# Modulation weights of a two-block network: from running weighted sums over input rows to dot products along the rows of outputs

## The chip, the cores and the metric

The kernel runs on one core of one Trainium2 chip, in float32 throughout. The metric is device time in microseconds (us) of one execution. Large products are made on TensorE with each weight split into a high part (`whi`, fp32r) and a low part (`wlo`); VectorE and ScalarE make the splits.

## The reference, cut to what matters

Two blocks follow each other. Each turns a condition vector into six vectors of 2048 numbers ("modulation": shifts, scales and gates), and uses them around its products. In the second block (the first is alike, with `w_ada`, `b_ada`):

```
sh_m, sc_m, gt_m, sh_f, sc_f, gt_f = split(silu(c) @ w_mod + b_mod, 6)
csh_m, csc_m, ...                  = split(silu(c_ctx) @ w_mod + b_mod, 6)
h_lat = rms_norm(x, norm_mix_g) * (1 + sc_m) + sh_m      # 256 latent tokens
h_ctx = rms_norm(ctx, norm_mix_g) * (1 + csc_m) + csh_m  # 256 context tokens
... mixer of h_lat and h_ctx ...
x = x + gt_m * (mixed @ w_out)
x = x + gt_f * swiglu(rms_norm(x, norm_ffn_g) * (1 + sc_f) + sh_f)
```

`w_ada` and `w_mod` are 2048 x 12288. Each is read once and multiplied with one or two vectors; from the context's condition only the first two of the six vectors are used. The mixer of block one is a state-space scan with pooling and Fourier branches, that of block two a gated linear scan (8 heads) and windowed attention (8 heads).

## The kernel before, in words

A planner (`schedule`) writes one list of "beats" for the whole program, and each engine runs the beats that name it, in that order. The main stream is the weights of the large products: SyncE loads pieces of 128x1024 (`raw`), ScalarE rounds each to `whi` (L1373), VectorE subtracts for `wlo` (L1800), and TensorE makes three matmuls per 128x128 block: `wlo`, `whi`, `whi` (L883). There are four `raw` buffers and three split buffers; a piece's split starts when the piece three before it has been used up. With a moving side of 256 columns a piece is 8 blocks.

Beside it runs a background stream, `mods`. `Plan.flowed` counts the columns that TensorE has been given and, whenever the background's pace is reached (4.7, 5.7, 4.2 and 6.0 in the four stages, in units close to a microsecond of TensorE), puts one step of `mods` into the list. What is said here holds for the 20 halves that it makes: in block one the vectors j = 2, 3, 4 (stage (0, 2), during the gates), then j = 5 (stage (0, 5), during the first feed-forward's gate and up products), in block two j = 0, 1 (stage (1, 0), until well into that feed-forward), j = 2, 3, 4 (stage (1, 2), during the scan and the attention) and j = 5 (stage (1, 5)). j = 0, 1 of block one are made at the start by other code, which the change leaves alone.

For each vector j and each half of its 2048 outputs, `mods` takes 16 pieces of 128 inputs x 1024 outputs. GpSimd loads each through its own queue (L847, a ring of two buffers). VectorE multiplies the piece by the 128 condition values that stand one per partition (`csil`, in `misc`), and adds it to an accumulator of 128x1024: `TENSOR_SCALAR` for the first (L1812), `SCALAR_TENSOR_TENSOR` for the other 15 (L1731, a helper's line). For j = 0, 1 of block two there are two conditions and so two accumulators: two instructions a piece. After the 16 pieces `modsum` sums over the partitions on TensorE: 8 products of a 128x128 block of the accumulator with one column of ones, into a PSUM tile of 128x8 ("ps<-cst,t ... 128x1"; the profile names its constant operand first, and shows two matmul records for each). VectorE adds the bias and writes `mv` (L1822, `modv<-ps,small`). `modsum` stands in TensorE's order like any other work, and what follows it there waits. Its PSUM tile comes from the ring `s.aux`, which has one bank in stages (0, 5) and (1, 0), two or four elsewhere.

ScalarE's part ahead of the change is only the `Silu` of the four condition vectors at the very start, on 128x16 each.

Of the kernel before, what the change touches and what calls it, by code (L numbers as in the profile page):

```python
# [11 lines left out]
P = 128  # L12
# [20 lines left out]
for _n, _w in [("b_ada", 96), ("norm_mix_w", 16), ("norm_ffn_w", 16), ("conv_w", 120), ("conv_b", 24),  # L33
               ("d_skip", 32), ("ssd_norm_w", 16), ("pool_scale", 16), ("final_norm_w", 16), ("c", 16),
# [3 lines left out]
    _small(_n, _w)  # L38
# [18 lines left out]

class Plan:


    def __init__(self):
# [3 lines left out]
        self.back, self.modded = iter(()), set()  # L65
# [81 lines left out]
def mods(s, layer, js):  # L147
    for j in js:
        for half in range(2):
            for k in range(KT):  # L150
                s.add("mod", layer, j, half, k)
                yield
            yield
            s.add("modsum", layer, j, half, s.aux)
        s.modded.add((layer, j))
        if j < 2:
            s.modded.add((layer, j + 6))
# [67 lines left out]
def schedule():  # L225
# [119 lines left out]
    def ctx2():  # L345
        s.need(1, 1)
# [216 lines left out]
class Dry:  # L563
# [6 lines left out]
    scalar_tensor_tensor = tensor_copy = reciprocal = memset = tensor_reduce = tensor_tensor_scan = dma_start = _none  # L570
# [16 lines left out]
def build(nc, A, out):  # L587
    ctx = ExitStack()
    with ctx:
# [4 lines left out]
        "rc_in rs_in am_in stored zero hi lo used pool_mm ada_pe ada_sum rms_pe mods_pe tr_pe dt_pe ssd_pe pf_pe hg_pe at_pe "  # L594
        "init_v ada_v mod_v start_v conv_v dt_v ssd_v pf_v merge_v res_v norm_v ffn_v hg_v at_v mat_v "
        "silu_a start_a sq_a conv_a tok_a dt_a ssd_a z_a pf_a gate_a norm_a ffn_a val_a hg_a at_a").split()


def program(nc, A, out, ctx):
# [23 lines left out]
    csil = misc[:, 16:80].rearrange("p (v k) -> p v k", v=4)  # L623
# [73 lines left out]
    mod_rings, accs = {}, {}  # L697

    def mod_memory(stage, after, n, n_acc):
        mod_rings[stage] = [Buf(carve(PIECE), f"w{i}", after) for i in range(n)]  # L700
        accs[stage] = [carve(PIECE) for _ in range(n_acc)]

    mod_memory((0, 2), f2, 2, 1)
# [13 lines left out]
    mod_memory((0, 5), f3, 2, 2)  # L717
    mod_rings[1, 0], accs[1, 0] = mod_rings[0, 5], accs[0, 5]
    c2sq = ring(1, lambda: carve(PIECE), f3)
# [6 lines left out]
    mod_memory((1, 2), f5, 2, 1)  # L726
# [36 lines left out]
    mod_memory((1, 5), f7, 2, 1)  # L763
# [9 lines left out]
    acc_bufs = {st: [Buf(a, None, f) for a in accs[st]] for st, f in (((0, 2), f2), ((0, 5), f3), ((1, 2), f5), ((1, 5), f7))}  # L773
    acc_bufs[1, 0] = acc_bufs[0, 5]
# [12 lines left out]

    def mod_stage(layer, j):
        return (layer, j) if (layer, j) in mod_rings else (layer, 2 if j > 1 else 0)
# [47 lines left out]
    def pool(e):  # L837
# [3 lines left out]
        def mod(layer, j, half, k):  # L841
            w = A["w_ada"] if layer == 0 else A["w_mod_2"]
            b = S.take(mod_rings[mod_stage(layer, j)], "mod", layer, j, half, k)
            S.free("mod", layer, j, half, k, by=("mod_v", "acc2" if j < 2 else "acc", layer, j, half, k))
            a = j * D + half * PIECE
            g.wait_ge(*S.freed("mod", layer, j, half, k))
            e.dma_start(b, w[k * P:(k + 1) * P, a:a + PIECE]).then_inc(*up(S.sem("mod", layer, j, half, k), layer, j, half, k, n=16))  # L847
# [28 lines left out]
        run(beats, {"mod": mod, "pf_load": pf_load, "ctx2": ctx2, "hg_in": hg_in})  # L876

    def pe(e):
# [156 lines left out]

        def modsum(layer, j, half, ring):
            for i in range(2 if j < 2 else 1):
                S.take(rings[ring], "mods", layer, j, half, i)
                acc = accs[mod_stage(layer, j)][i]
                g.wait_ge(*S.freed("mods", layer, j, half, i), *at("mod_v", "acc2" if i else "acc", layer, j, half, KT - 1))  # L1040
                ps = S.buf("mods", layer, j, half, i)
                for m in range(8):
                    ins = mm(ps[:, m:m + 1], acc[:, m * P:(m + 1) * P], ones[:, 0:1])
                ins.then_inc(*up("mods_pe", layer, j, half, i))
# [273 lines left out]
        run(beats, {"ada": ada, "ada_sum": ada_sum, "ada_tr": ada_tr, "rms_in": rms_in, "mm": product, "pool": pooled, "modsum": modsum, "btok": btok, "xtok": xtok, "dt": dt, "ssd": ssd,  # L1318
# [3 lines left out]
    def act(e):  # L1322
# [14 lines left out]
        for v, name in enumerate(("c", "c_ctx", "c_2", "c_ctx_2")):  # L1337
# [381 lines left out]
        run(beats, {"rms_in": rms_in, "ada_sum": ada_sum, "ada_h": ada_h, "stage": stage, "silu": silu, "btok": btok, "xtok": xtok, "ev_dt": ev_dt, "dt": dt, "ssd": ssd, "ev_z": ev_z,  # L1719
# [5 lines left out]
    def dve(e):  # L1725
# [76 lines left out]
        def mod(layer, j, half, k):  # L1802
            b, st = S.buf("mod", layer, j, half, k), mod_stage(layer, j)
            g.wait_ge(*at(S.sem("mod", layer, j, half, k), layer, j, half, k))
            for i in range(2 if j < 2 else 1):
                acc, cv, key = accs[st][i], csil[:, 2 * layer + i, k:k + 1], ("acc", "acc2")[i]
                if k == 0:
# [683 lines left out]
```

## Time and profile before

| | |
|---|---|
| median of 3 runs | 3573.88 us (3573.77 to 3575.22) |
| the profiled execution | 3571.92 us, span 3570.1 us |
| busy: TensorE | 3438.3 us, 96% of the span |
| busy: VectorE | 2375.5 us, 67% |
| busy: ScalarE | 1540.5 us, 43% |
| busy: GpSimd | 180.1 us, 5% |
| granted TensorE clock, mean | 0.984 of full speed |

PE is TensorE's matmuls, PEld its weight loads, DVE is VectorE, ACT ScalarE, POOL GpSimd, SP SyncE. The span starts with the first instruction and ends with the last; 1.8 us of the execution lie outside it.

### The profile page before, as it was taken

How to read it: one execution, taken by the hardware profiler on the slowest of the kernel's cores; microseconds unless marked ns; L12 is line 12 of the kernel's file. 1: busy time of each engine (PE TensorE's matmuls, PEld its weight loads, DVE VectorE, ACT ScalarE, POOL GpSimd, SP SyncE). 2: the span in 40 equal slices, each digit the busy share in tenths (PEclk: the TensorE clock that was granted, in tenths of full speed). 3: DMA queues.
4: the chain of work that ended last, by engine and by line, in shares of the span. 5: the costliest groups of instructions: out<-in, count | busy, mean ns of one | idle time of the engine just before them, and what ended most of it. 6: DMA issues, size and time to landing. Idle time of an engine off the chain costs nothing. (4 is left out here: it accounts for less than half of the span.)

```text
span 3570.1 us, 59053 instructions
## 1 busy us (share of the span) xinstructions
PE 3438.3 (96%) x25176; PEld 3196.5 (90%) x25176; DVE 2375.5 (67%) x3028; ACT 1540.5 (43%) x2174; POOL 180.1 (5%) x342
## 2 busy tenths in 40 slices
PE   7889999899999999999999999999988999999999
PEld 3477788699999989999999989999887899999999
DVE  6876666456777776688776566766696666445544
ACT  2244545434333344433433444555454444334443
POOL 0000000000001000000000001001000000000000
PEclk8999999999999999999999999999999999999999
DMA  7632223467888767777777556556552577655555
GB/s 286 239 113 77 83 95 130 165 217 269 273 282 280 240 225 263 263 258 257 251 244 231 169 165 225 193 172 205 183 178 98 193 254 258 179 187 185 188 182 174
DMA packets 199702, 725.64 MB, mean 203 GB/s; under 512 B 22160, under 2 KB 22416, under 8 KB 198928
## 3 DMA queue, kind: packets, MB, share of 16 engines
q1 hardware_dynamic: 150912, 540.71, 44.8%
q0 software_dynamic: 47808, 176.18, 15.5%
q8 instruction: 198, 3.24, 0.4%
q10 hardware_dynamic: 720, 4.98, 0.4%
q14 instruction: 64, 0.52, 0.0%
HBM read 719.69 MB, written 2.10 MB: 202 GB/s over the span
## 5 line engine op out<-in xcount | busy, mean ns | idle before, releaser
L883 PE MATMUL ps<-hT,whi 128*128 128x256 f32 (+1 forms) x11360 | 2201.4, 294 | 0.0
L883 PEld LDWEIGHTS ps<-hT,whi 128*128 128x128 f32 x11360 | 1795.8, 189 | 58.1 <-issue 6.5
L883 PE MATMUL ps<-hT,wlo 128*128 128x256 f32 (+1 forms) x5680 | 1708.6, 301 | 57.4 <-DVE wlo L1800 22.2
L1800 DVE TENSOR_TENSOR wlo<-raw,whi 128x1024 fp32r<-128x1024 f32 (+1 forms) x978 | 1176.8, 1207 | 820.7 <-ACT whi L1373 819.7
L1373 ACT ACTIVATE whi<-raw 128x1024 fp32r<-128x1024 f32 (+1 forms) x978 | 1016.3, 1042 | 946.7 <-PE ps L883 937.0
L883 PEld LDWEIGHTS ps<-hT,wlo 128*128 128x128 f32 x5680 | 1075.9, 189 | 115.1 <-issue 76.6
L883 PE MATMUL ps<-t,whi 128*128 128x256 f32 x3136 | 568.5, 282 | 0.0
L1731 DVE SCALAR_TENSOR_TENSOR t<-t,misc 128x1024 f32<-128x1024 f32 (+2 forms) x504 | 550.1, 1119 | 19.5 <-DMA t<-in_w_mod 15.0
L883 PEld LDWEIGHTS ps<-t,whi 128*128 128x128 f32 x3136 | 487.2, 190 | 0.4
L883 PE MATMUL ps<-t,wlo 128*128 128x256 f32 x1568 | 448.2, 286 | 3.8 <-DVE wlo L1800 3.8
L883 PEld LDWEIGHTS ps<-t,wlo 128*128 128x128 f32 x1568 | 294.8, 188 | 4.8 <-DVE wlo L1800 4.2
L883 PE MATMUL ps<-t 128*128 128x256 f32 (+4 forms) x992 | 203.7, 352 | 18.2 <-ACT t L1713 9.3
L883 PEld LDWEIGHTS ps<-t 128*128 128x128 f32 x992 | 149.0, 194 | 53.1 <-issue 20.2
L883 PE MATMUL ps<-whi,hT 128*128 128x256 f32 (+1 forms) x896 | 191.1, 312 | 0.0
L847 POOL DMA_DIRECT2D t<-in_w_mod x192 | 102.0, 531 | 1224.9 <-DVE t L1731 948.1
L883 PEld LDWEIGHTS ps<-whi,hT 128*128 128x128 f32 x896 | 145.3, 189 | 12.7 <-issue 1.4
L883 PE MATMUL ps<-wlo,hT 128*128 128x256 f32 (+1 forms) x448 | 144.2, 322 | 7.0 <-DVE wlo L1800 6.0
L1530 ACT ACTIVATE t<-t 128x256 fp32r<-128x256 f32 x88 | 36.9, 419 | 226.8 <-DVE t L2123 226.8
L883 PE MATMUL ps<-t,cst 128*128 128x256 f32 (+1 forms) x318 | 92.0, 412 | 19.4 <-DVE t L1731 6.4
L847 POOL DMA_DIRECT2D t<-in_w_ada x128 | 67.8, 530 | 748.9 <-DVE t L1731 569.9
L883 PEld LDWEIGHTS ps<-wlo,hT 128*128 128x128 f32 x448 | 84.8, 189 | 15.2 <-DVE wlo L1800 7.0
L1523 ACT ACTIVATE t<-ps 128x256 f32<-128x256 f32 x88 | 33.9, 385 | 142.6 <-PE ps L883 142.6
(220 smaller groups left out, 1560.1 us busy)
## 6 DMA issues: line engine op xcount, KB each, us to landing
raw<-in_w_in_s SPq DMA_DIRECT2D x250, 512.0 KB, 4.6
t<-in_w_mod POOLq DMA_DIRECT2D x192, 512.0 KB, 4.9
raw<-in_w_ffn_gu SPq DMA_DIRECT2D x176, 512.0 KB, 5.1
raw<-in_w_gu SPq DMA_DIRECT2D x176, 512.0 KB, 4.4
t<-in_w_ada POOLq DMA_DIRECT2D x128, 512.0 KB, 5.3
t<-in_w_ada_s SPq DMA_DIRECT2D x64, 512.0 KB, 4.5
raw<-in_w_out SPq DMA_DIRECT2D x64, 512.0 KB, 4.4
raw<-in_w_ffn_down SPq DMA_DIRECT2D x64, 512.0 KB, 4.2
```

What stands on the lines that cost most here:

```text
L847: e.dma_start(b, w[k * P:(k + 1) * P, a:a + PIECE]).then_inc(*up(S.sem("mod", layer, j, half, k), layer, j, half, k, n=16))
L883: return e.matmul(o, l, r, start=start, stop=stop)
L1373: fn(S.buf("split", p)[0][:, 0:n], S.buf("raw", p)[:, 0:n], ACT.Copy).then_inc(*up("hi", p))
L1523: fn(S.buf("gf", layer, m), S.buf("ps", t)[:, 0:T], ACT.Silu).then_inc(*up("ffn_a", "g", layer, m))
L1530: fn(F[layer]["hid"][0][:, i, :], S.buf("gf", layer, m), ACT.Copy).then_inc(*up("ffn_a", "hid", layer, m))
L1731: return e.scalar_tensor_tensor(out=o, in0=a, scalar=s, in1=b, op0=op0, op1=op1)
L1800: tt(lo[:, 0:n], S.buf("raw", p)[:, 0:n], hi[:, 0:n].bitcast(F32), ALU.subtract).then_inc(*up("lo", p))
```

## The change

The modulation weights are laid out on the host so that a piece holds 128 outputs on the partitions and 1024 inputs along the free dimension. The condition (1024 inputs, the same on all partitions) is loaded as a 128x1024 tile from a new input `conds`, and ScalarE applies `Silu` to it in place (`cond_silu`, L1363). VectorE then makes one `tensor_tensor_reduce` per piece and condition (L1838): product with the condition, sum along the free dimension, starting from the bias in the first half of the inputs and from `mv` in the second. The sum lands in one column of `mv`. The product itself is written back over the piece or, for the first of two conditions, into `c2sq`, a tile that nothing reads then. The accumulators, the `modsum` beats, their PSUM tiles and the additions of the bias are gone. A vector is now finished when both halves of its inputs have been seen, not half by half of its outputs. The conditions need 14 tile loads in all, on GpSimd's queue, and 14 `Silu`s of 128x1024. A `cond` step and a `cond_silu` step each take beats of the background stream in which no piece is used; the two `Silu`s of the second block's conditions at the start are dropped.

```
 def mods(s, layer, js):
-    for j in js:
-        for half in range(2):
-            for k in range(KT):
-                s.add("mod", layer, j, half, k)
-                yield
-            yield
-            s.add("modsum", layer, j, half, s.aux)
-        s.modded.add((layer, j))
...
+    both = CONDS[mod_stage(layer, js[0])]
+    nv = 2 if js[0] < 2 else 1
+    if nv == 2:
+        order = [(j, 0) for j in js] + [(j, 1) for j in js[::-1]]
+    else:
+        order = [(j, (n + i) % 2 if both < 2 else i) for n, j in enumerate(js) for i in range(2)]
+    held, seen = [None] * (both // nv), set()
+    for j, half in order:
+        if half not in held:
...
+                for v in range(nv):
+                    s.add("cond", layer, v, h, j)
+            yield
+            yield
+            for h in held:
+                for v in range(nv):
+                    s.add("cond_silu", layer, v, h, j)
...
+            yield
+        for m in range(KT):
+            s.add("mod", layer, j, half, m, j not in seen, tuple(s.cond[layer, v, half] for v in range(nv)))
+            yield
...
# ScalarE
+        def cond_silu(layer, v, half, j):
+            b = S.buf("cond", layer, v, half, j)
+            g.wait_ge(*at(S.sem("cond", layer, v, half, j), layer, v, half, j))
+            fn(b, b, ACT.Silu).then_inc(*up("cond_a", layer, v, half, j))
...
# TensorE
-        def modsum(layer, j, half, ring):
...
-                for m in range(8):
-                    ins = mm(ps[:, m:m + 1], acc[:, m * P:(m + 1) * P], ones[:, 0:1])
...
# VectorE
-                if k == 0:
...
-                    ins = ts(acc, b, cv, None, ALU.mult)
-                else:
...
-                    ins = stt(acc, b, cv, acc, ALU.mult, ALU.add)
...
-                tt(mv[:, layer, j + 6 * i, 8 * half:8 * half + 8], S.buf("mods", layer, j, half, i)[:, 0:8],
-                   sm(bias, j * 16 + 8 * half, 8), ALU.add).then_inc(*up("mod_v", "mv" if half else "mv0", layer, j + 6 * i))
...
+        def mod(layer, j, half, m, first, cond):
...
+            for v, n in enumerate(cond):
+                o = mv[:, layer, j + 6 * v, m:m + 1]
...
+                e.tensor_tensor_reduce(c2sq[0].t if v < len(cond) - 1 else b, b, S.buf("cond", layer, v, half, n), 1.0,
+                                       sm(bias, j * 16 + m, 1) if first else o, ALU.mult, ALU.add, o).then_inc(*up("mod_v", v, layer, j, half, m))
```

VectorE's order where pieces with two conditions are used, in the first feed-forward. Before, each piece gives two `SCALAR_TENSOR_TENSOR` into the accumulators:

```order
L2123 TENSOR_TENSOR t<-ps,t 128x256
L2126 TENSOR_TENSOR t<-t 128x256
L1800 TENSOR_TENSOR wlo<-raw,whi 128x1024 x2
L1731 SCALAR_TENSOR_TENSOR t<-t,misc 128x1024 x2
L1800 TENSOR_TENSOR wlo<-raw,whi 128x1024 x2
L1731 SCALAR_TENSOR_TENSOR t<-t,misc 128x1024 x2
```

And after the change at the same kind of place (`ISA t,modv<-...` is the product with its sum, `ISA modv 128x1` the instruction that writes the sum out):

```order
L2140 TENSOR_TENSOR t<-ps,t 128x256
L2143 TENSOR_TENSOR t<-t 128x256
L1823 TENSOR_TENSOR wlo<-raw,whi 128x1024 x2
L1838 ISA t,modv<-t,modv 128x1024
L1838 ISA modv 128x1
L1838 ISA t,modv<-t,modv 128x1024
L1838 ISA modv 128x1
L1823 TENSOR_TENSOR wlo<-raw,whi 128x1024 x2
```

Each accumulation has become a pair of instructions; the work around it stands as it stood.

TensorE's order at the end of the first block's mixer, ahead of the feed-forward's first product. Before:

```order
L883 MATMUL ps<-hT,whi 128x256 x2
L883 MATMUL ps<-t,cst 128x256 x2
L883 MATMUL ps<-cst,t 128x1 x8
L883 MATMUL ps<-hT,wlo 128x256
L883 MATMUL ps<-hT,whi 128x256 x2
```

And after the change:

```order
L911 MATMUL ps<-hT,whi 128x256 x2
L911 MATMUL ps<-t,cst 128x256 x2
L911 MATMUL ps<-hT,wlo 128x256
L911 MATMUL ps<-hT,whi 128x256 x2
```

The eight one-column products are gone, here and at the 19 other places where `modsum` stood (four of them hold two sets, 16 products).

ScalarE's order at the start of the second block's scan stage, where its modulation starts. Before:

```order
L1373 ACTIVATE whi<-raw 128x1024
L1579 ACT_TABLE_LOAD
L1579 ACTIVATE t<-ps 128x512
L1373 ACTIVATE whi<-raw 128x1024 x2
L1579 ACTIVATE t<-ps 128x512
L1585 ACT_TABLE_LOAD
```

And after the change (L1363 is the `Silu` of a condition tile):

```order
L1396 ACTIVATE whi<-raw 128x1024
L1602 ACT_TABLE_LOAD
L1602 ACTIVATE t<-ps 128x512
L1396 ACTIVATE whi<-raw 128x1024 x2
L1363 ACT_TABLE_LOAD
L1363 ACTIVATE t<-t 128x1024
L1602 ACT_TABLE_LOAD
L1602 ACTIVATE t<-ps 128x512
L1608 ACT_TABLE_LOAD
```

One `Silu` and two table loads have come in between two evictions. Over the whole program ScalarE has five table loads more (105 against 100).

## Rows read from the trace of the kernel before

**Rows 1.** The page: busy time by engine.

```profile
PE 3438.3 (96%) x25176; PEld 3196.5 (90%) x25176; DVE 2375.5 (67%) x3028; ACT 1540.5 (43%) x2174; POOL 180.1 (5%) x342
```

**Rows 2.** Windows of some stages: PE, PEld, DVE, ACT, POOL busy, PEclk, DMA share, GB/s.

```profile
800.00:1000.00 200.00, 199.40 (x1686) 198.78 (x1685) 140.66 (x145) 80.33 (x95) 19.08 (x36) 1.00 0.81 273
1500.00:1925.00 425.00, 424.11 (x3532) 423.86 (x3531) 344.46 (x346) 165.66 (x196) 33.39 (x63) 0.98 0.76 255
2577.00:2640.00 63.00, 53.99 (x366) 48.59 (x365) 57.45 (x81) 32.91 (x57) 4.24 (x8) 0.95 0.54 177
```

**Rows 3.** TensorE's group of one-column products, from the groups by shape.

```profile
L883 PE MATMUL ps<-cst,t 128*128 128x1 f32 x384 | 46.2, 250 | 1.2 <-DVE modv L1822 1.1
```

**Rows 4.** TensorE in order of time around a single `modsum` (stage (0, 2)).

```profile
828.21 1.84 PE L883 MATMUL ps<-cst,t 128*128 128x1 f32 x16
829.91 0.37 PE L883 MATMUL ps<-t,wlo 128*128 128x256 f32 x1
...
830.36 0.28 PE L883 MATMUL ps<-t,wlo 128*128 128x256 f32 x1
```

**Rows 5.** TensorE in order of time at a double `modsum` (stage (1, 0)).

```profile
1928.00 1.84 PE L883 MATMUL ps<-cst,t 128*128 128x1 f32 x16
...
1931.90 0.36 PE L883 MATMUL ps<-hT,wlo 128*128 128x256 f32 x1
```

**Rows 6.** Windows behind two of the double ones; columns as in Rows 2.

```profile
1715.00:1719.00 4.00, 4.00 (x24) 4.00 (x24) 0.97 (x2) 0.82 (x1) 0.53 (x1) 0.60 0.45 150
1821.00:1825.00 4.00, 4.00 (x19) 4.00 (x20) 1.00 (x3) 0.00 (x0) 0.00 (x0) 0.50 0.36 124
```

**Rows 7.** VectorE in order of time in stage (1, 0), one gate/up cycle.

```profile
1899.67 1.23 DVE L1800 TENSOR_TENSOR wlo<-raw,whi 128x1024 fp32r<-128x1024 f32 x1 [0.53 <-ACT whi L1373]
...
1904.83 1.23 DVE L1800 TENSOR_TENSOR wlo<-raw,whi 128x1024 fp32r<-128x1024 f32 x1 [0.40 <-ACT whi L1373]
...
1911.35 1.23 DVE L1800 TENSOR_TENSOR wlo<-raw,whi 128x1024 fp32r<-128x1024 f32 x1 [0.52 <-ACT whi L1373]
```

**Rows 8.** VectorE's groups by shape: busy us, mean ns; the nearest to the new instructions.

```profile
L1800 DVE TENSOR_TENSOR wlo<-raw,whi 128x1024 fp32r<-128x1024 f32 x914 | 1115.6, 1224 | 783.2 <-ACT whi L1373 782.2
L1731 DVE SCALAR_TENSOR_TENSOR t<-t,misc 128x1024 f32<-128x1024 f32 x360 | 455.5, 1279 | 15.8 <-DMA t<-in_w_mod 15.0 <-DMA t<-in_w_ada 0.5
L2190 DVE TENSOR_TENSOR_SCAN t<-cst,t 128x256 f32<-128x256 f32 x32 | 19.5, 673 | 4.2 <-ACT t L1585 4.2
L2066 DVE TENSOR_TENSOR t<-t 128x256 f32<-128x256 f32 x32 | 13.6, 425 | 1.1
L2323 DVE TENSOR_REDUCE t<-t 128x1 f32<-128x512 f32 x16 | 11.0, 686 | 0.6
L2332 DVE RECIPROCAL t<-t 128x1 f32<-128x1 f32 x16 | 2.6, 164 | 0.6
```

**Rows 9.** ScalarE in order of time, attention: a sum that is written out.

```profile
2608.52 0.72 ACT L1706 ACTIVATE t<-t 128x512 f32<-128x512 f32 x1 [2.76 <-DVE t L2325]
2609.15 0.19 ACT L1706 ACTIVATION_READ_ACCUMULATOR t<-t 128x1 f32 x1
2609.24 0.28 ACT L1707 ACTIVATE t<-small,t 128x1 f32<-128x1 f32 x1
```

**Rows 10.** ScalarE's groups by shape; a load of GpSimd's queue (KB, us to landing).

```profile
L1373 ACT ACTIVATE whi<-raw 128x1024 fp32r<-128x1024 f32 x914 | 962.8, 1056 | 896.6 <-PE ps L883 886.9 <-DMA raw<-in_w_in_t 9.4
L1379 ACT ACT_TABLE_LOAD x12 | 15.4, 1283 | 0.2
t<-in_w_mod POOLq DMA_DIRECT2D x192, 512.0 KB, 4.9
```

**Rows 11.** VectorE, then TensorE, in order of time where stage (1, 2) starts.

```profile
2124.11 0.75 DVE L1812 TENSOR_SCALAR t<-t,misc 128x1024 f32<-128x1024 f32 x1 [3.60 <-DMA t<-in_w_mod]
...
2137.76 0.36 PE L883 MATMUL ps<-hT,wlo 128*128 128x256 f32 x1 [4.76 <-DVE wlo L1800]
```

More of the change, by code:

```diff
@@ L64, in __init__ @@
         self.pace, self.flow = [2.0, 5.0], [0.0, 0.0]
-        self.back, self.modded = iter(()), set()
+        self.back, self.modded, self.cond = iter(()), set(), {}
         self.lins, self.aux = "lin3", "aux_b"
@@ L345, in ctx2 @@
     def ctx2():
-        s.need(1, 1)
+        s.need(1, 0)
         for i in range(13):
@@ L696, in program, with mod_memory @@
     gt = ring(4, lambda: carve(T), f2)
-    mod_rings, accs = {}, {}
-    def mod_memory(stage, after, n, n_acc):
+    mod_rings, cond_rings = {}, {}
+    def mod_memory(stage, after, n):
         mod_rings[stage] = [Buf(carve(PIECE), f"w{i}", after) for i in range(n)]
-        accs[stage] = [carve(PIECE) for _ in range(n_acc)]
-    mod_memory((0, 2), f2, 2, 1)
+        cond_rings[stage] = [Buf(carve(PIECE), f"cond{i}", after) for i in range(CONDS[stage])]
+    mod_memory((0, 2), f2, 2)
     merged = carve3(16, T)
@@ L874, in hg_in @@
             ins.then_inc(*up("zero"))
-        run(beats, {"mod": mod, "pf_load": pf_load, "ctx2": ctx2, "hg_in": hg_in})
+        run(beats, {"mod": mod, "cond": cond, "pf_load": pf_load, "ctx2": ctx2, "hg_in": hg_in})
     def pe(e):
@@ L1316, in attend @@
             ins.then_inc(*up("at_pe", "ao", h))
-        run(beats, {"ada": ada, "ada_sum": ada_sum, "ada_tr": ada_tr, "rms_in": rms_in, "mm": product, "pool": pooled, "modsum": modsum, "btok": btok, "xtok": xtok, "dt": dt, "ssd": ssd,
+        run(beats, {"ada": ada, "ada_sum": ada_sum, "ada_tr": ada_tr, "rms_in": rms_in, "mm": product, "pool": pooled, "btok": btok, "xtok": xtok, "dt": dt, "ssd": ssd,
                     "pool_fourier": pool_fourier, "ev_res": ev_res, "ctx2": ctx2, "norm2": norm2, "hgrn": hgrn,
@@ L1336, in act @@
         g.wait_ge(*at("small_in"))
-        for v, name in enumerate(("c", "c_ctx", "c_2", "c_ctx_2")):
+        for v, name in enumerate(("c", "c_ctx")):
             fn(csil[:, v, :], sm(name), ACT.Silu).then_inc(*up("silu_a", v))
@@ L1818, in modsum @@
-        def modsum(layer, j, half, _):
-            bias = "b_ada" if layer == 0 else "b_mod_2"
-            for i in range(2 if j < 2 else 1):
-                g.wait_ge(*at("mods_pe", layer, j, half, i), *at("small_in"))
-                tt(mv[:, layer, j + 6 * i, 8 * half:8 * half + 8], S.buf("mods", layer, j, half, i)[:, 0:8],
-                   sm(bias, j * 16 + 8 * half, 8), ALU.add).then_inc(*up("mod_v", "mv" if half else "mv0", layer, j + 6 * i))
-                S.free("mods", layer, j, half, i, by=("mod_v", "mv" if half else "mv0", layer, j + 6 * i))
+        unread = []
@@ new lines, in mod @@
+        def mod(layer, j, half, m, first, cond):
+            b, bias = S.buf("mod", layer, j, half, m), "b_mod_2" if layer else "b_ada"
+            g.wait_ge(*at("small_in"), *at(S.sem("mod", layer, j, half, m), layer, j, half, m))
+            for v, n in enumerate(cond):
+                o = mv[:, layer, j + 6 * v, m:m + 1]
+                g.wait_ge(*at("cond_a", layer, v, half, n))
+                if v < len(cond) - 1:
+                    g.wait_ge(*(at("mod_v", 0, *unread) if unread else at(*f3)))
+                    unread[:] = layer, j, half, m
+                if not first:
+                    g.wait_ge(*at("mod_v", v, layer, j, 1 - half, m))
+                e.tensor_tensor_reduce(c2sq[0].t if v < len(cond) - 1 else b, b, S.buf("cond", layer, v, half, n), 1.0,
+                                       sm(bias, j * 16 + m, 1) if first else o, ALU.mult, ALU.add, o).then_inc(*up("mod_v", v, layer, j, half, m))
+                if not first and m == KT - 1:
+                    M.table["mod_v", "mv", layer, j + 6 * v] = M.table["mod_v", v, layer, j, half, m]
```

81 lines of the change are left out of this document (38 added, 43 removed), and 1 row of the table SMALL.

## The prediction

> **What bounds the kernel now.** I read the page first: TensorE is busy 3438 of 3570 us, VectorE 2376, ScalarE 1541, GpSimd 180 [rows 1]. A share over the whole says little, so windows by stage came next. Where the background stream runs beside large products, TensorE has no gap: 199.4 of 200 us in the gates, 424.1 of 425 us in the stretch where pieces have two conditions, while VectorE has 141 of 200 and 344 of 425 [rows 2]. There each us taken off TensorE is a us of the kernel, so long as VectorE keeps delivering `wlo`. Only the attention stage looks different: VectorE 57.5 of 63 us, TensorE 54.0 [rows 2]. So the question is what the change takes from TensorE, and whether VectorE's dearer or cheaper instructions show through.
>
> **What goes from TensorE.** Twenty halves are made: 16 with one condition and 4 with two, so 24 sets of 8 one-column products. Their records sum to 46.2 us [rows 3]. How much of that is the path, the order of time tells. At a single `modsum` the products start at 828.21, where the next product of the stream would have started; that one starts at 829.91, and the block after it at 830.36 [rows 4]. Blocks follow each other every 0.355 us (8 of them, 2.84 us, are one piece), so without the products the block after it would have started at 828.57: 1.79 us each, and 16 of them give 28.6 us. At a double one the stream stands from 1928.00 to 1931.90 [rows 5], and starts 0.1 us slower: the second set waits for the bank that VectorE must free, because the ring has one. Four of these are 16 us.
>
> Behind the double ones the granted clock goes from 2.4 GHz to the lower level of 1.2 GHz for a few us; of the four places two are shown: 0.60 over 1715 to 1719, 0.50 over 1821 to 1825 [rows 6]. What TensorE did before it fell were the 128x1 products and the short wait between the two sets. Over 1500 to 1925 the clock is 0.98 [rows 2]; the windows add up to some 8 us of products that ran at half speed. With the products gone I count these 8 us as given back; the lower bound is 0, if the clock falls for another reason. Sum: 28.6 + 16 + 8 = 53 us off, 45 without the clock.
>
> **What VectorE pays.** Before: 360 `SCALAR_TENSOR_TENSOR` of 1279 ns and 24 first ones [rows 8]; two in a row last 2.48, so one takes 1.20 us of the queue. After: 384 pairs. The new main instruction appears nowhere in the trace. From below it is the two-input `TENSOR_TENSOR` (1224 ns), from above I first take the `SCALAR_TENSOR_TENSOR` (1279), since it too has two float32 tensors and a per-partition scalar. `TENSOR_REDUCE` sums 512 in 686 ns [rows 8], one element per cycle, so a running sum need not cost more. Its second half, the instruction that writes out the sum, has its nearest row on ScalarE: there `ACTIVATION_READ_ACCUMULATOR` lasts 0.19 us but the next instruction starts 0.09 us after it [rows 9]. On VectorE the dearest thing of that size is the `RECIPROCAL` of 128x1, 164 ns [rows 8]. If the reader also has to wait until the main one is over (0.08 us past its 1.20), a pair is at most 1.20 + 0.08 + 0.17 = 1.45 us, at least 1.14. Call x what a pair takes beyond 1.20: between -0.06 and 0.25. I take 0.12, nearer ScalarE's row since its reader is the same kind of instruction.
>
> x times 384 would be 46 us, almost all of it under TensorE. Where is there no cover? In stage (1, 0). One gate/up cycle of the feed-forward holds 4 pieces. VectorE starts one at 1899.67 and the next at 1911.35 [rows 7]: 11.68 us for a cycle that held two pairs, of which it stood 0.40 waiting for `whi` and about 1.0 in a dependent wait on ScalarE (0.52 of it is in the last row). TensorE needs 4 x 2.84 = 11.36 us for such a cycle. On average the pace (5.7 units, 6.06 us) puts 1.87 pieces, 3.75 instructions, into it: 4 x 1.14 for `wlo`, 3.75 x 1.20, and 1.85 for the two evictions with their waits make 10.9 us. The slack is 0.46 us a cycle, used up at x = 0.12. Beyond, TensorE waits 3.75x - 0.46 us in each of about 26 cycles: 12 us at x = 0.25. At 0.12 I put 2 us for uneven cycles.
>
> In the attention VectorE is nearly the bound. The beats now leave three empty steps there for a new condition tile, so by the fifth head 9 pieces have been used instead of 13, and four come later, under output products. I put +1.5 us, between -3 and +4.
>
> **What ScalarE and the queues pay.** 14 `Silu` of 128x1024 cost 1.06 us each, as `whi` does, and 5 table loads 1.28 us: 21 us on an engine that is 43% busy [rows 1, 10]. They stand in nine places in its order, singly or in pairs, behind at most one load and before another, and the next `whi` is behind them. A piece's split starts when the third before it is used up and must be ready two pieces later, 5.68 us; 1.06 + 1.23 are the split itself, some 1.2 VectorE's queue. That leaves 2.2 us, a pair with its load is 3.4 us: up to 1.2 us of wait in each of the nine, much of it in ScalarE's idle time. I take 3 us, between 0 and 10. The wait of `cond_silu` for its tile holds the same `whi`: 4.9 us to landing [rows 10], and the two empty steps ahead of it are 8 to 12 us, so it is hidden; GpSimd, whose queue issues the tile, is idle 95% of the time [rows 1]. 14 more loads are 7 MB on 726.
>
> At the start of stage (1, 2) VectorE today waits for the first piece, 3.6 us at 2124 [rows 11], while a `wlo` stands behind. Now that wait is ScalarE's, for the condition tile, and its eviction stands behind. TensorE's gap of 4.76 us at 2137.76 [rows 11] comes after a chain through both. I put -1, between -4 and +3.
>
> **Sum.** -53 + 2 + 1.5 + 3 - 1 = -47.5 us. The profiled execution took 3571.9 us (span 3570.1 plus 1.8), 2 us under the median; the difference, taken from the median 3573.9 it is 3526, a span of about 3523.
>
> **Rivals.**
> (a) The sum along the row runs at half rate. The trace has such an instruction: the scan, which carries a value from element to element, takes 673 ns for 256 where `TENSOR_TENSOR` takes 425 [rows 8], two cycles an element. By that slope 1024 are 2.23 us, so x = 1.13. Then a gate/up cycle is over by 3.78 us, 98 us in 26 cycles; the down products in the same stretch (16 outputs of 7.8 us, VectorE at 6.7 with 2.58 instructions each) are over by 1.8 us each, 29; attention adds 10. -53 + 98 + 29 + 10 + 0 = +84: 3658 us. It starts to cost at x = 0.12, and the kernel becomes slower than before from about x = 0.5. Against: `TENSOR_REDUCE` is at full rate. For: nothing here shows product and sum in one. Chance 12%.
> The Trainium skill says as much in "Vector Engine (DVE) Microarchitecture Reference", section "Points that are easy to get wrong": the instruction layout of `scalar_tensor_tensor`, with two SBUF sources that are not bf16, halves its throughput, as no port is left for the accumulator. By that rule the old instructions should be at half rate too; the trace does not agree, with 1279 ns for 1024 float32 elements from two SBUF tiles. Whether it holds for an instruction that does sum, no run here shows yet.
> (b) Covers fail in small things: x near 0.25, ScalarE's insertions at their full 10 us, the clock not given back. -45 + 12 + 4 + 10 + 3 = -16; short of all at once, -30 to -16: 3544 to 3558. Chance 17%.
> (c) The one-column products were hidden: the time stays within 7 us. Against it stands the rhythm at 828 us. Chance 4%.
> (d) More than counted: x below 0, better starts of stages, under 3513. Chance 6%.
>
> **How the numbers follow.** The forecast (3513 to 3544) has 61%. Its own bounds: -53 - 3 - 4 = -60 at best, about 3514; at the other end half of each upper bound, 3544. Taking in (b) to 3560 leaves (a), (c) and a little of (d) outside: 3513 to 3560. A measurement of this kernel can tell 0.2%, 7 us. Faster: 61 + 17 + 6 = 84%. Same 4%. Slower 12%.
>
> **What the profile after would show.** Right: no "128x1" products of `cst`; TensorE's instructions down by 384; blocks at 0.355 us straight through what were the `modsum` places; clock 1.00 through the two-condition stretch; the new instructions at 1.2 to 1.3 us and a reader of 0.06 to 0.2; VectorE's busy time up by some 40 to 60 us. TensorE's waits on `wlo` in that stretch should stay at a few us in all. Wrong: readers or sums that cost more, seen as VectorE over 95% busy between 1500 and 1900 and regular gaps of TensorE "<-DVE wlo"; or gaps behind the nine places of `cond_silu`. The weakest number is x.

## The result and the profile after

The changed kernel takes 3486.86 us (median of 4 executions, 3481.81 to 3498.93) against 3573.82 (3569.70 to 3575.22) for the kernel before: a ratio of 0.9768, 95% interval 0.9751 to 0.9786, some 83 to 87 us less. I had forecast 3526 and a range down to 3513: the sign was right, and nearly half of the gain was not in the sum.

The page and the windows that answer to [rows 1, 2, 6], of the changed kernel (columns as there):

```profile
PE 3342.8 (96%) x24792; PEld 3094.5 (89%) x24792; DVE 2386.6 (69%) x3388; ACT 1561.8 (45%) x2191; POOL 187.5 (5%) x356
```

```profile
800.00:1000.00 200.00, 198.89 (x1729) 198.28 (x1728) 150.69 (x192) 83.59 (x99) 21.20 (x40) 1.00 0.85 294
1500.00:1925.00 425.00, 424.94 (x3582) 423.91 (x3581) 351.54 (x470) 177.30 (x213) 35.04 (x67) 1.00 0.79 267
1715.00:1719.00 4.00, 4.00 (x36) 4.00 (x35) 4.00 (x5) 1.06 (x1) 0.53 (x1) 1.00 0.77 260
```

TensorE has 384 instructions less, as announced, but its busy time fell by 95.5 us, twice what the products of [rows 3] can explain. VectorE's rose by 11 us, not by the 40 to 60 that I had written. The two-condition stretch has a granted clock of 1.00, also where [rows 6] had 0.60. VectorE's groups by shape in the changed kernel, beside [rows 8]:

```profile
L1823 DVE TENSOR_TENSOR wlo<-raw,whi 128x1024 fp32r<-128x1024 f32 x914 | 1114.9, 1224 | 714.9 <-ACT whi L1396 711.7
L1838 DVE CUSTOM_DVE_ANT_0 t<-t,modv 128x1024 f32<-128x1024 f32 x192 | 243.3, 1280 | 9.5 <-DMA t<-in_w_mod 8.6 <-DMA t<-in_w_ada_r 0.7
L1838 DVE CUSTOM_DVE_ANT_0 t<-t,small 128x1024 f32<-128x1024 f32 x192 | 243.3, 1280 | 13.9 <-DMA t<-in_w_mod 12.2 <-DMA t<-in_w_ada_r 1.5
L1838 DVE DVE_READ_ACCUMULATOR2_ANT modv<- 128x1 f32 x384 | 32.3, 84 | 0.0
```

And in order of time, the second sum of a piece, its reader, and a `wlo` behind them:

```profile
1700.70 1.28 DVE L1838 CUSTOM_DVE_ANT_0 t<-t,modv 128x1024 f32<-128x1024 f32 x1
1701.90 0.09 DVE L1838 DVE_READ_ACCUMULATOR2_ANT modv<- 128x1 f32 x1
1701.90 1.23 DVE L1823 TENSOR_TENSOR wlo<-raw,whi 128x1024 fp32r<-128x1024 f32 x1
```

The reader starts in the same hundredth as the next instruction, 1.20 us after the main one: x, what a pair takes beyond 1.20 us, is 0. The sum runs at full rate, 1280 ns for 1024 elements. So where are some 40 us more? TensorE in order of time where the code of both kernels is the same, the products of the last feed-forward that move `hT`. The kernel before:

```profile
3200.23 0.40 PE L883 MATMUL ps<-hT,whi 128*128 128x256 f32 x2
3200.46 0.28 PE L883 MATMUL ps<-hT,wlo 128*128 128x256 f32 x1
3200.58 0.40 PE L883 MATMUL ps<-hT,whi 128*128 128x256 f32 x2
3200.82 0.28 PE L883 MATMUL ps<-hT,wlo 128*128 128x256 f32 x1
```

The changed kernel:

```profile
3200.18 0.39 PE L911 MATMUL ps<-hT,whi 128*128 128x256 f32 x2
3200.40 0.28 PE L911 MATMUL ps<-hT,wlo 128*128 128x256 f32 x1
3200.52 0.39 PE L911 MATMUL ps<-hT,whi 128*128 128x256 f32 x2
3200.74 0.28 PE L911 MATMUL ps<-hT,wlo 128*128 128x256 f32 x1
```

A block of three matmuls took 0.353 us and now takes 0.340. Nothing waits in either, and both have the full granted clock, 2.4 GHz. Windows show it without reading single starts: PE busy, its instructions, granted clock, DMA share, GB/s. Two windows of the kernel before:

```profile
1300.00:1500.00 200.00, 200.00 (x1703) 1.00 0.79 267
3200.00:3300.00 100.00, 100.00 (x852) 1.00 0.56 187
```

and four of the changed one:

```profile
1300.00:1500.00 200.00, 200.00 (x1767) 1.00 0.82 280
1700.00:1800.00 100.00, 100.00 (x851) 1.00 0.80 271
2850.00:2950.00 100.00, 100.00 (x885) 1.00 0.83 280
3200.00:3300.00 100.00, 100.00 (x884) 1.00 0.59 195
```

In the kernel before, 2850 to 2950 holds 852 as well. A window also counts the matmuls that only reach over its edges, two or three more than fit in. So the counts serve to compare windows of one length, and the time from one matmul to the next is taken below from the starts in the traces: 117.8 ns before and 113.3 after in these stretches, which is a third of the 0.353 and 0.340 us. Not all of the changed kernel is quick: from some 1630 to 1877 us, the later gate and up products of the first feed-forward, it has the old rhythm (851).

The instructions there are the same. The diff drops two entries of 16 columns each from the table of small constants, so `small`, which is allocated between the split tiles and `cst`, is 128 bytes per partition shorter. `raw`, `whi` and `wlo` lie ahead of it and stay; `hT` and everything behind it move down by 128 bytes. In the compiled program `whi0` starts at byte 32896 of each partition (128 modulo 256, and so do all `raw`, `whi` and `wlo`), `hT0` at 63424 before (192) and at 63296 after (64), the tiles of the hidden activations at 224 before and 96 after. Below, **distance** is the address of the operand that moves less that of the stationary weights, modulo 256: for `hT` 64 before, 192 after; for the hidden activations 96 before, 224 after. It follows from the widths alone: from `whi0` to `hT0` are six split tiles of 4096 bytes, `small` (589 columns before, 557 after, rounded up to 2368 and 2240 bytes), `cst` with 2560 and `modv` with 1024, in all 30528 bytes before and 30400 after. In a row of the profile the operand that moves stands first (`ps<-hT,wlo`: `hT` moves); so it is in "ps<-cst,t" too, where the column of ones moves.

### The profile page after: what moved, and what is told of

It reads as the page before. It is cut to its first block and busy times, and to the rows that moved or that the text cites. A ratio compares the mean times of both kernels' runs of the same rounds, so it can differ in the third digit from the quotient of the medians.

```text
span 3480.0 us, 58548 instructions
## 1 busy us (share of the span) xinstructions
PE 3342.8 (96%) x24792; PEld 3094.5 (89%) x24792; DVE 2386.6 (69%) x3388; ACT 1561.8 (45%) x2191; POOL 187.5 (5%) x356
## 5 line engine op out<-in xcount | busy, mean ns | idle before, releaser
L911 PE MATMUL ps<-hT,whi 128*128 128x256 f32 (+1 forms) x11360 | 2153.3, 292 | 0.0
L911 PE MATMUL ps<-hT,wlo 128*128 128x256 f32 (+1 forms) x5680 | 1698.0, 299 | 59.0 <-DVE wlo L1823 23.7
L911 PE MATMUL ps<-t,whi 128*128 128x256 f32 x3136 | 559.6, 281 | 0.0
L1838 DVE CUSTOM_DVE_ANT_0 t<-t,small 128x1024 f32<-128x1024 f32 x192 | 243.3, 1280 | 13.9 <-DMA t<-in_w_mod 12.2
L1838 DVE CUSTOM_DVE_ANT_0 t<-t,modv 128x1024 f32<-128x1024 f32 x192 | 243.3, 1280 | 9.5 <-DMA t<-in_w_mod 8.6
L868 POOL DMA_DIRECT2D t<-in_w_ada_r x128 | 67.8, 530 | 629.8 <-DVE modv L1838 623.1
```

The source lines that it names most:

```text
L868: e.dma_start(b, src).then_inc(*up(S.sem("mod", layer, j, half, m), layer, j, half, m, n=16))
L911: return e.matmul(o, l, r, start=start, stop=stop)
L1838: e.tensor_tensor_reduce(c2sq[0].t if v < len(cond) - 1 else b, b, S.buf("cond", layer, v, half, n), 1.0, sm(bias, j * 16 + m, 1) if first ...
```

## The experiments

**Is it the address?** Theory A: the change's own edits give what I had summed, and the rest comes from the 128 bytes. Theory B: addresses do nothing. Two kernels cross the two, a third takes the products out alone.

`after_high`, the changed kernel at the old addresses:

```
-NSMALL = sum(w for _, w in SMALL.values())
+NSMALL = sum(w for _, w in SMALL.values()) + 32
```

> The changed kernel with its tile of small constants padded by 32 unused columns, so that every tile behind it has the partition address that it had in the kernel before; no instruction differs. Theory A (the change gave some 45 us by its own edits, and the rest because the moving operands of TensorE's matmuls now lie 128 bytes lower, where a 128x256 matmul starts every 113.3 ns and not every 117.8): 3526 to 3532 us, steps of 117 to 118 ns wherever hT moves. Theory B (addresses do not matter; the gates' matmuls run faster because the pauses of the modulations' sums are gone): 3487 us, as the changed kernel.

Measured: 3527.78 us, ratio to before 0.9876 (0.9861 to 0.9891). Theory A, to 2 us of the forecast of 3526.

`before_low`, the kernel before at the new addresses:

```
-    small = sb("small", NSMALL)
+    small = sb("small", NSMALL - 32)
...
+        e.dma_start(modv[:, 128:160], A["small"][:, NSMALL - 32:NSMALL])
```

> The kernel before with a tile of small constants that is 32 columns narrower (the two conditions of the second layer come by a transfer of their own into a tile that was there), so that every tile behind it lies 128 bytes lower, as in the changed kernel; all the work stays, the products of the sums too. Theory A (address): 3574 less some 40 us, about 3530 (3522 to 3540), with steps of about 114 ns where hT moves. Theory B (no effect of the address): 3574.

Measured: 3534.23 us, ratio 0.9896 (0.9881 to 0.9910). So 38.6 us come from tiles that lie 128 bytes lower; the work is the same but for one small transfer of its own at the start. The windows of `before_low`:

```profile
3200.00:3300.00 100.00, 100.00 (x884) 1.00 0.58 195
3065.00:3095.00 30.00, 30.00 (x256) 30.00 (x255) 14.60 (x16) 11.29 (x12) 0.00 (x0) 1.00 0.62 183
```

884 in 100 us again where `hT` moves, as after; in the second window (columns as in [rows 2]), where the hidden activations move, 256, against 252 in the kernel before.

`before_1col`, the kernel before with one product of eight columns for eight of one:

```
-                for m in range(8):
-                    ins = mm(ps[:, m:m + 1], acc[:, m * P:(m + 1) * P], ones[:, 0:1])
+                ins = mm(ps[:, 0:8], acc[:, 0:P], ones[:, 0:8])
```

> The kernel before, where the eight one-column products of each modulation sum are one product: it leaves out seven of the eight column sums, and keeps the wait for the sum, VectorE's work and all addresses. What the column products themselves cost TensorE: seven eighths of 24 sums at about 1.1 to 1.5 us of columns each is 23 to 32 us: 3542 to 3551 us if the wait for the sum's end and the products are both paid as counted in the prediction. If the gain of the change came from the products alone (theory C: they cost more than they show, through the clock or the rhythm of the matmuls that follow): under 3520.

Measured: 3534.72 us, ratio 0.9894 (0.9879 to 0.9909): 38.1 us, more than the 23 to 32 expected. I had left the clock out of that expectation. Its order of time at a double place, to be read beside [rows 5], and its window over the two-condition stretch:

```profile
1905.99 0.28 PE L883 MATMUL ps<-cst,t 128*128 128x8 f32 x2
1906.79 0.39 PE L883 MATMUL ps<-cst,t 128*128 128x8 f32 x2 [0.52 <-DVE modv L1821]
1907.04 0.36 PE L883 MATMUL ps<-hT,wlo 128*128 128x256 f32 x1
1907.24 0.40 PE L883 MATMUL ps<-hT,whi 128*128 128x256 f32 x2
```

```profile
1500.00:1925.00 425.00, 421.07 (x3538) 420.70 (x3537) 346.34 (x350) 170.14 (x203) 32.86 (x62) 1.00 0.77 259
```

Without the one-column and eight-column products, the traces of `before`, `before_1col` and `after_high` hold the same 24792 matmuls in the same order, so their starts can be compared one by one. Across the 16 single places `before_1col` gains 1.4 to 1.6 us each (0.7 at the one among the attention's heads), across the four double ones 4.6, 1.6, 5.3 and 4.4: 39.6 us in all, where the two profiled executions differ by 37.6. `after_high` gains 1.8 at a single place and 5.5, 5.6, 7.2 and 5.5 at the double ones, as the prediction had counted (1.79, and 4 with 2 for the clock).

The clock is 1.00 over this stretch where the kernel before had 0.98 [rows 2] (and `before_low`, which keeps the products, has 0.98 too), but the mean hides one drop. At the second double place the second set waited much longer for its bank, and the clock fell after it:

```profile
1697.36 0.39 PE L883 MATMUL ps<-cst,t 128*128 128x8 f32 x2 [1.93 <-DVE modv L1821]
```

```profile
1698.00:1702.00 4.00, 4.00 (x25) 0.62 0.63 190
```

At the other three the waits were 0.26, 1.22 and 0.52 us, and the clock stayed at 1.00. In the kernel before, the waits between the sets were only 0.26 to 0.37 us and it fell at all four places, so there the products themselves brought it down; but a wait can do it without them. Single sets of 8 one-column products did not: the clock is 1.00 over 800 to 1000 [rows 2], with two of them inside.

**Address or distance?** 16 unused columns in `small` put `hT` at 128 modulo 256, the weights' own residue: `after_p16`, edit as above with `+ 16`.

> The changed kernel with the tile of small constants padded by 16 unused columns: all behind it moves up by 64 bytes, so that hT starts at 128 modulo 256 and the tiles of the attention output and of the hidden activations at 160. Theory A has no rule yet for which addresses are quick; in the kernel before whi and wlo, at 128 modulo 256, moved at 113.5 to 114.3 ns, so it expects hT quick: 3475 to 3500. Theory B: 3487.

Measured: 3546.88 us, ratio 0.9925 (0.9909 to 0.9942). My guess of a quick `hT` was wrong: it is the worst place of all. The same 16 columns ahead of the very first tile, `after_all16`, put `hT` at the same residue and move the weights too:

```
+    sb("pad", 16)
     raw_t = [sb(f"raw{i}", PIECE)[:, :] for i in range(NRAW)]
```

> The changed kernel with 16 unused columns ahead of the first tile of all, raw0: every tile moves up by 64 bytes, the weights (raw, whi, wlo) as well as hT and the tiles behind it. hT then starts at 128 modulo 256, where the kernel with 16 columns in the small constants had steps of 119.9 ns, but the distance between the weights and hT stays that of the changed kernel. Theory A1 (the distance between the stationary and the moving operand decides): 3487 us (3480 to 3494), hT steps of 114.4. Theory A2 (the moving operand's own address decides): about 3547, steps of 119.9 in hT.

Measured: 3497.36 us, ratio 0.9782 (0.9764 to 0.9800); 10 us over the middle of what A1 said, and 50 from A2. The windows of `after_p16`, then of `after_all16`:

```profile
2850.00:2950.00 100.00, 100.00 (x836) 1.00 0.78 265
3200.00:3300.00 100.00, 100.00 (x836) 1.00 0.55 184
```

```profile
2850.00:2950.00 100.00, 100.00 (x851) 1.00 0.79 270
3200.00:3300.00 100.00, 100.00 (x885) 1.00 0.57 194
```

With `hT` at the same residue one makes 836 matmuls (119.9 ns each) and the other 885. The distance decides, not the operand's own address. (All `raw`, `whi` and `wlo` have one residue, so a distance to `raw`, which the transfers write and VectorE reads, would fit as well; no run parts the two.) But the second kernel shows something more: at distance 192 one stretch runs at 851 and another at 885. From 1300 to 1500 it holds 1701, where the changed kernel has 1767. Two such stretches of some 250 us, 4% slower, are 18 us; its profiled execution was 13 us longer than that of the changed kernel, its median 10.

**The map of distances.** Two kernels set the tiles' residues with unused columns and a narrower `misc`; `after_t64` touches the later tiles alone, `after_hT0` puts `hT` at 0 (distance 128) and the later tiles at 64.

```
-    misc = sb("misc", 200)
+    misc = sb("misc", 192)
...
-    lbv = misc[:, 168:200]
+    lbv = misc[:, 160:192]
```

> The changed kernel with the tile misc narrower by 8 unused columns: hT stays, the tiles behind misc (attention output, hidden activations) move down by 32 bytes, from 96 to 64 modulo 256, the residue at which hT moves at 114.4 ns while they take 118.3. Some 4700 matmuls move them. Theory A: their step falls to 114 to 115, so 15 to 19 us less: 3468 to 3473. Theory B (what sets the step of these is that they read other tiles, or VectorE's load, and not the address): 3487.

> The changed kernel with 48 unused columns ahead of the small constants' successor and misc packed to 144 columns: hT at 0 modulo 256, 128 away from the weights, the tiles behind misc at 64. A residue not yet seen for hT. If the step depends on the distance modulo 256 and is worst at 0 (119.9), a distance of 128 is the farthest and may be the quickest: 112 to 114 ns, 3455 to 3473. If only the distance of minus 64 is quick: steps near 118, 15000 of them 3.5 ns slower than in the changed kernel less the gain of the tiles at 64: about 3520.

Measured: `after_t64` 3482.55 us, ratio 0.9763 (0.9705 to 0.9821), but in two groups: 3462.80 and 3463.61, 3501.48 and 3502.09. `after_hT0` 3518.98, ratio 0.9853 (0.9835 to 0.9871): 128 is not the quickest, though the farthest.

Then a version whose constants are in two tiles, cut at a chosen column with the larger part behind `res`, so that `hT` can be set without the tiles behind `misc` (unused columns and a narrower `misc` keep those at a distance of 192):

```
-    small = sb("small", NSMALL)
+    small = sb("small", CUT)
...
+    rest = sb("rest", NSMALL - CUT)
```

> The changed kernel with the small constants split in two tiles, the larger one put behind the tiles of hT and res, and misc packed: hT now lies 448 bytes modulo 512 beyond the weights, the hidden activations too. So far hT was seen at distances of 192, 256, 320 and 384 modulo 512, and only at 192 did it move in steps of 113 ns. If the pattern repeats every 256 bytes, this is the same as 192: hT at 114 to 115 ns, 3463 to 3502, as the kernel with its later tiles at 64. If it repeats every 512 bytes, 448 is new for hT; the hidden activations of the second layer took 113.4 ns there in every block, so hT would do as well in every block: 3440 to 3460.

> The same, with hT at a distance of 0 modulo 512 (256 was the worst, 119.9 ns). Repeating every 256 bytes: steps of 119.9 ns, 15000 of them 5.5 ns over those of the changed kernel, less what the later tiles gain: 3540 to 3550. Repeating every 512: another value, the time unknown, under 3520 if 0 is the opposite of the worst.

> The same, with hT at a distance of 64 modulo 512 (320 gave 117.8 ns, and was the place in the kernel before). Repeating every 256 bytes: 117.8 ns, 50 us over the quick times: 3505 to 3520. Repeating every 512: another value, as 192 and 448 could differ.

> The same, with hT at a distance of 128 modulo 512 (384 gave 118.7 ns). Repeating every 256 bytes: 118.7 ns and 3519, as the kernel with hT at 0 modulo 256. Repeating every 512: another value.

Measured: `after_d448` 3492.18 us (3466.83 to 3502.71), ratio 0.9763 (0.9720 to 0.9806); `after_d0` 3528.42, 0.9874 (0.9860 to 0.9889), 12 to 22 us under what I wrote. The later tiles gained what I had put (three stretches of 1056 matmuls at 113.4 instead of 118.3 ns, 16 us), so what I had too high was `hT`'s part: I had taken every `hT` step of the changed kernel as quick, and the stretch from 1630 to 1877 (851, above) was not. `after_d64`: 3509.98, 0.9822 (0.9802 to 0.9842). `after_d128`: 3519.42, 0.9851 (0.9834 to 0.9867). The window 3200 to 3300, in this order:

```profile
3200.00:3300.00 100.00, 100.00 (x885) 1.00 0.57 193
```

```profile
3200.00:3300.00 100.00, 100.00 (x836) 1.00 0.55 185
```

```profile
3200.00:3300.00 100.00, 100.00 (x852) 1.00 0.55 186
```

```profile
3200.00:3300.00 100.00, 100.00 (x845) 1.00 0.54 185
```

Each count is that of the distance that is 256 bytes away (885 and 884; 836; 852; 845 in `after_hT0`), so for these four the pattern repeats every 256 bytes. `after_d160` tries the last untried one for all tiles, with `CUT` at 96, 8 unused columns and `misc` of 176.

> hT and the later tiles at a distance of 160 modulo 256 from the weights. The distances of 32, 96 and 224 gave 117.5, 120.4 and 118.3 ns for the later tiles. By their neighbours (128: 118.8; 192: 113.3 or 117.8) about 118.5 ns and 3515 to 3530; under 3460 if 160 is quick in every stretch.

Measured: 3541.73 us, ratio 0.9903 (0.9891 to 0.9916), 12 us longer than the upper end expected: not quick anywhere. Together, the counts of the windows, with the ns from start to start of the same stretches:

| distance, modulo 256 | `hT` moves, 3200 to 3300 | hidden activations move, 3065 to 3095 |
|---|---|---|
| 0 | 836 (120.0 ns) | |
| 32 | | 257 (117.8) |
| 64 | 852 (117.8) | |
| 96 | | 252 (120.0) |
| 128 | 845 (118.7) | |
| 160 | 855 (117.3) | 258 (117.3) |
| 192 | 885 (113.3) | 267 (113.3) |
| 224 | | 256 (118.3) |

At 160 and 192, the distances that both kinds of tile had, both have the same step. At three distances a stretch can also run in a longer rhythm: at 192 in 117.8 ns (`after_all16`), and at 128 and 160 in 120.1 and 118.8 ns, as `after_d128` and `after_d160` show:

```profile
1300.00:1500.00 200.00, 200.00 (x1669) 1.00 0.78 267
```

```profile
1300.00:1500.00 200.00, 200.00 (x1688) 1.00 0.80 271
```

where twice the 100 us windows above would give 1690 and 1710.

The row of `after_t64` for the best entry:

```profile
3065.00:3095.00 30.00, 30.00 (x267) 30.00 (x267) 15.22 (x16) 11.97 (x13) 0.00 (x0) 1.00 0.63 198
```

**Why one kernel has two times.** The quickest version and the changed kernel, both run again unchanged.

> The kernel with the later tiles at 64 modulo 256 once more, unchanged, for its spread: times in two groups, near 3463 and near 3501, if a whole stretch (gates, gate/up products, the last feed-forward) falls into one rhythm or the other at its start and stays there; a spread without groups if each block chooses anew.

> The changed kernel once more, unchanged: four executions lay between 3482 and 3499. If stretches fall into a rhythm by chance, some executions will have the gate/up products of the first layer quick (3475 to 3485) and others slow (3495 to 3500); against the kernel above in the same call it tells what the 32 bytes of the later tiles are worth: 17 us at the median, by their 4700 matmuls, or nothing if their rhythm is as often the slow one.

Measured: `after_t64_2` 3462.80 us (3459.62, 3461.68, 3462.00, 3463.60, 3471.27, 3494.63), ratio 0.9708 (0.9682 to 0.9735); `after_2` 3492.05 (3488.78 to 3495.74), ratio 0.9769 (0.9756 to 0.9781). The intervals don't meet: the 32 bytes of the later tiles are worth 0.6%, 22 us by the ratios (29 by the medians). With the four of `after_t64` taken in, ten executions of this version have a mean of 3474.3 us, eight of the changed kernel 3490.4: 16 us, which is what 3 x 1056 steps of 118.3 instead of 113.3 ns make. This version is the fastest found, 3.1% under the kernel before by the median of `after_t64_2`. The windows of `after_2`, to be read beside those of the changed kernel above (the same program):

```profile
1300.00:1500.00 200.00, 200.00 (x1767) 1.00 0.81 278
2850.00:2950.00 100.00, 100.00 (x852) 1.00 0.79 268
3200.00:3300.00 100.00, 100.00 (x885) 1.00 0.57 192
```

885 matmuls in one execution, 852 in the other, from 2850 to 2950. In the records that whole half of the second layer's gate/up products (some 250 us) is in one rhythm, and those around it hardly differ; 4% of 250 us is 10, the difference of the two profiled times (3491.52 and 3481.81). So at distance 192 a stretch runs at 113.3 or at 117.8 ns, and mostly holds what it has. What picks one was not found.

**How much slack has VectorE?** `after_slow` adds a reduction ahead of each sum:

```
+                e.tensor_reduce(misc[:, 2:3], S.buf("cond", layer, v, half, n)[:, 0:512], AX.X, ALU.max)
```

> The changed kernel with one more VectorE instruction ahead of each of the 384 sums, a TENSOR_REDUCE of 512 elements (686 ns, about 0.63 us of the queue) whose result nobody reads. It tests the slack that the prediction gave VectorE: x = 0.63. By its working the gate/up cycles are over by 3.75 x 0.63 - 0.46 = 1.9 us each, 49 us in 26; the down products by 6.7 + 2.58 x 0.63 - 7.8 = 0.5 us each, 8; the attention 5: 62 us, 3549. If VectorE has more slack than I counted (the pace evens out over cycles, other stretches hide it all): under 3515. If it has none: 384 x 0.63 = 242 us, 3729.

Measured: 3571.97 us (3560.98 to 3584.04), ratio 1.0001 (0.9987 to 1.0015): 85 us over the changed kernel, 62 expected. The two-condition stretch, and TensorE's groups that wait for `wlo` (the changed kernel has 23.7, 4.0 and 7.3 us in the last figures):

```profile
1500.00:1925.00 425.00, 392.50 (x3232) 383.21 (x3231) 391.96 (x554) 157.28 (x188) 32.19 (x61) 0.99 0.69 240
```

```profile
L911 PE MATMUL ps<-hT,wlo 128*128 128x256 f32 (+1 forms) x5680 | 1709.2, 301 | 97.9 <-DVE wlo L1823 60.0
L911 PE MATMUL ps<-t,wlo 128*128 128x256 f32 x1568 | 447.0, 285 | 13.4 <-DVE wlo L1823 13.3
L911 PE MATMUL ps<-wlo,hT 128*128 128x256 f32 (+1 forms) x448 | 145.8, 325 | 10.3 <-DVE wlo L1823 9.3
```

The profiled executions, 3578.12 and 3481.81 us, differ by 96 us. The waits rose from 35.0 to 82.6 us, 48 of these. Besides, the windows 1300 to 1500 and 2850 to 2950 hold 1700 and 852 instead of 1767 and 885: 4% of two stretches, each some 240 us, about 19, and these come from the two rhythms and not from VectorE's work, as far as the runs tell. The attention (below) took 7 us more. The last 22 are not accounted for. So 242 us of extra VectorE work cost about a third of itself, and by the starts half of the 96 us arose where the prediction placed it, between 1504 and 1894 us of the changed kernel.

## Why the prediction was wrong

**The step that failed** is one that isn't in the sum. I counted what instructions are removed, added and moved, and took the remaining matmuls at the old rhythm, so that their term was 0 without a reason: "blocks at 0.355 us straight through". The diff also shortens the table of small constants by 32 columns. I had its line before me, and treated it as a matter of names; I had read block after block at 0.355 us, and took that for what a block costs. Layout alone gives 38.6 us on the kernel before (0.9896), and the step from `after_high` to the changed kernel is 1.08% by the ratios, again 38.6 (that the two agree so closely is chance: executions of the changed kernel lie up to 17 us apart). The change's own edits give 45 us (3572.84 to 3527.78 in the same runs), where I had -47.5. 45 + 38.6 is the measured gain of some 83 us.

**Products: right, but for one place.** I had -45 for the places and -8 for the clock. From `before` to `after_high` the starts show 26.7 us over 15 single places and 23.8 over the four double ones, 50.5 in all; 7.8 of the 23.8 are what goes beyond 4 us a place, the clock's share. The sixteenth single place, at 2682.6 us, lies among the attention's heads, and there it was not on the path: `before_1col` needs the same 128.2 us for the heads. The clock over 1500 to 1925 is 1.00 in all kernels without the products but `after_slow` (0.99), whose TensorE waits there.

**VectorE: right in place, too dear by 2 us.** x is 0, not 0.12, and no term is left of it: TensorE's waits for `wlo` in `after_high` are 22.0 + 3.8 + 5.6 us, in the kernel before 22.2 + 3.8 + 6.0. Rival (a), the sum at half rate, is out by the 1280 ns. The rule of the Trainium skill that stood beside it ("Vector Engine (DVE) Microarchitecture Reference", "Points that are easy to get wrong") halves the throughput of `scalar_tensor_tensor`'s layout for two SBUF sources that are not bf16. The trace of the kernel before does not agree, with 1279 ns for 1024 float32 elements, and the new instruction, which the rule does not name, takes the same 1280.

**Attention: mis-sized.** I put +1.5 us, at most +4. The sixteen exponentials of the heads start from 2608.5 to 2736.6 us in the kernel before, 128.1 us, and from 2557.1 to 2692.8 in `after_high`, 135.7: 7.6 us more, with the same in the changed kernel (2537.5 to 2673.3). TensorE's starts tell where: from 2612 to 2682 us of the kernel before the two run level to 0.3 us, and by 2730 us 7.1 are lost. In that last part the kernel before has no piece of the background stream left, while `after_high` still uses six. The last accumulation before, then the first and the last of these six:

```profile
2674.47 1.28 DVE L1731 SCALAR_TENSOR_TENSOR t<-t,misc 128x1024 f32<-128x1024 f32 x1
```

```profile
2637.86 1.28 DVE L1838 CUSTOM_DVE_ANT_0 t<-t,modv 128x1024 f32<-128x1024 f32 x1
2677.33 1.28 DVE L1838 CUSTOM_DVE_ANT_0 t<-t,modv 128x1024 f32<-128x1024 f32 x1
```

Six pieces at 1.20 us of the queue are 7.2 us. I had four pieces come late, and thought them under the output products; they are six, and under the last heads, where VectorE is nearly the bound. The condition's `Silu` (2562.2 us in `after_high`) stands where nothing is lost. No run moves the pieces alone, so this rests on the two traces.

**ScalarE: smaller than counted.** The 14 `Silu` take 1051 ns each, as counted, but TensorE's waits for `wlo`, which follows `whi`, did not grow, by the figures above: near 0, not +3.

**Start of stage (1, 2): right in kind, too small.** TensorE's gap of 4.76 us [rows 11] is 1.33 us in `after_high`, in one row:

```profile
2098.63 0.36 PE L911 MATMUL ps<-hT,wlo 128*128 128x256 f32 x1 [1.33 <-DVE wlo L1823]
```

-3.4 us, not -1. Sum of the terms as measured, between the two profiled executions: -50.5 + 0 + 7.1 + 0 - 3.4 = -46.8, where these differ by 47.8 (the medians by 45). The rest is small and goes both ways: `after_high` is 2.4 us behind ahead of its first place. That the forecast of the edits came out at 2 us is partly luck: products and attention were off by 2.5 and 5.6 us one way, and VectorE, ScalarE and the start of the stage by 7.4 together the other way.

**Rivals.** (c), hidden products, is out by `before_1col`. (b) didn't come. (d), "more than counted", had 6% for x below 0 and better starts; the time came out there, but by a cause that was on no list.

## What to carry to other kernels

Where TensorE is the bound and never waits, measure its step between equal matmuls in a full window (count by time) before you believe that it is what the matmul costs, and compare the address residues of what moves with those of the weights. Any edit that changes the width of an early tile moves all later ones; compare it with a version padded back to the old addresses before crediting the edit, and read the diff's allocations as closely as its instructions. Here 128 bytes were worth nearly as much as the rewriting (39 us and 45); with the later tiles at distance 192 as well, six of ten executions take 3460 to 3464 us.

## What the hardware showed that I had not expected

For 128x256 float32 matmuls in this kernel, at the full granted clock, the step from one to the next depends on the byte distance in a partition between moving and stationary operand, modulo 256: 120.0 ns at 0, 117.8 at 64, 118.7 at 128, 117.3 at 160 and 113.3 at 192. At 128, 160 and 192 a longer rhythm (120.1, 118.8, 117.8) may hold for a stretch instead. All steps of 32 bytes were seen, but not each with `hT`, and none between.

Which way round the distance is to be taken is not settled. In three short stretches of stage (1, 2), of 192 matmuls each, the weights move and `hT` stays. Taken as above, the distance there is 192 in the kernel before, and its two unbroken stretches run at 113.4 ns. In the changed kernel it is 64, and two of the stretches run at 113.3 ns and one at 117.8; of the latter, one of each kind:

```profile
2137.00:2157.00 20.00, 20.00 (x179) 1.00 0.84 291
2242.00:2262.00 20.00, 20.00 (x172) 1.00 0.75 264
```

Where `hT` moves at 64, no long stretch was quick in any trace. Whether the cause is how weights and moving data are read in turn is not shown by any run.

Two sets of one-column products, 4 us together with a wait of 0.26 to 0.37 us between them, pulled the granted clock from 2.4 GHz to 1.2 for a few us; a single set of 1.8 us did not. With one product of eight columns for each set (48 records against 384) the clock fell at one double place of four, the one with a wait of 1.93 us.
